# Rotary rotation run beside a projection's weight splits, keys turned in the retention's opening, and four side column tiles moved to the delta solve

## The reference, cut to what matters

```python
def rope(x, pos):
    ...
    x1, x2 = x[..., :half], x[..., half:]
    return jnp.concatenate([x1 * cos - x2 * sin, x2 * cos + x1 * sin], axis=-1)

q_b = rope(q_b.reshape(B, L, H_B, DK_B).astype(f32), pos)
k_b = rope(k_b.reshape(B, L, H_B, DK_B).astype(f32), pos) * (DK_B ** -0.5)
o_b, s_ret_new = retention(q_b, k_b, v_b, s_ret)
...
merged = (jax.nn.sigmoid(sel_a) * jnp.einsum('blv,vd->bld', o_a, w_br_a)
          + jax.nn.sigmoid(sel_b) * jnp.einsum('blv,vd->bld', o_b, w_br_b))
```

## Time and profile before

| | |
|---|---|
| median of 3 runs | 2276.4 us (2275.66 to 2284.68) |
| the profiled execution | 2275.99 us, its span 2274.1 us |
| PE busy | 1841.2 us, 81% of the span |
| DVE busy | 1303.4 us, 57% |
| ACT busy | 889.5 us, 39% |
| POOL busy | 639.1 us, 28% |
| DMA | 636.74 MB, mean 280 GB/s |

### The profile page before, as it was taken

One profiled execution on the slowest core, in us unless ns is written; L12 is line 12 of the kernel. 1 busy time (PEld: TensorE's weight loads), 2 busy tenths in 40 slices (PEclk: granted clock), 3 DMA queues, 4 the chain that ended last, 5 costly groups with the idle time before them and its releaser, 6 DMA issues.

```text
span 2274.1 us, 25972 instructions
## 1 busy us (share of the span) xinstructions
PE 1841.2 (81%) x8664; PEld 1184.0 (52%) x8664; DVE 1303.4 (57%) x2807; ACT 889.5 (39%) x2294; POOL 639.1 (28%) x558
## 2 busy tenths in 40 slices
PE   5989779979886986899997777777778777877776
PEld 4988679969766985655552222222223222322221
DVE  2227254451365524677667667676676867767664
ACT  4223212332224324354444544434444444444444
POOL 0002011000100002345444433444333444444442
PEclk9999789979897997999999999999999999999999
DMA  3313112253114235799999999999999999999997
GB/s 101 122 42 92 29 36 63 71 185 107 28 56 168 93 112 150 294 416 417 417 393 421 418 421 421 420 419 417 402 421 420 410 420 419 398 421 421 421 416 300
DMA packets 171783, 636.74 MB, mean 280 GB/s; under 512 B 12530, under 2 KB 97589, under 8 KB 104712
## 3 DMA queue, kind: packets, MB, share of 16 engines
q0 software_dynamic: 74880, 545.29, 58.1%
q1 hardware_dynamic: 96784, 89.98, 12.7%
HBM read 617.39 MB, written 17.93 MB: 279 GB/s over the span
## 4 chain that ended last, share of the span: by engine, by line
DMA 30%; PE 13%; DVE 8%; ACT 7%; issue 2%; POOL 0%; ACTq 0%; DVEq 0%
DMA ex_uv_row<-in_peer_uv,ex_eidx 30%; PE ps L1930 10%; DVE ex_uv_row L2093 4%; ACT L1976 2%; ACT ex_spread L1984 2%; ACT L1970 1%; ACT ret_tables L1981 1%; PE ps L571 1%; PE ps L573 1%; PE ps L572 1%; ACT ret_tables L1976 1%; DMA ex_uv_row<-in_peer_uv,ex_eidx_s 1%; DVE ex_sel L2065 0%; DVE ex_sel L2069 0%; DVE ex_best L2068 0%
## 5 line engine op out<-in xcount | busy, mean ns | idle before, releaser
L1930 PE MATMUL ps<-ex_uv_row,ex_spread 128*128 128x512 f32 (+1 forms) x2080 | 985.5, 609 | 264.1 <-ACT ex_spread L1984 260.4
L2093 DVE CUSTOM_DVE_ANT_0 ex_uv_row<-ex_uv_row,x_ffn 128x1024 f32<-128x1024 f32 x512 | 624.7, 1225 | 403.7 <-DMA ex_uv_row<-in_peer_uv,ex_eidx 398.9
L1930 PEld LDWEIGHTS ps<-ex_uv_row,ex_spread 128*128 128x128 f32 (+1 forms) x2080 | 363.1, 189 | 849.6 <-issue 849.4
L1892 POOL DMA_INDIRECT ex_uv_row<-in_peer_uv,ex_eidx x512 | 552.7, 1079 | 782.1 <-PE ps L1930 726.6
L1976 ACT ACTIVATE ret_tables<-ret_tables 128x1 f32<-128x1 f32 x520 | 104.7, 201 | 637.2 <-DVE ret_tables L2093 636.0
L1984 ACT ACTIVATE ex_spread<-square,ret_tables 128x128 f32<-128x128 f32 (+1 forms) x520 | 208.0, 400 | 17.0
L1981 ACT ACTIVATE ret_tables<-ret_tables 128x1 f32<-128x1 f32 x512 | 150.6, 294 | 17.0
L571 PE MATMUL ps<-proj_b_whi,x_lo 128*128 128x256 f32 (+1 forms) x320 | 91.1, 285 | 8.8 <-DVE proj_b_wlo L512 8.8
L571 PE MATMUL ps<-x_hi,ex_w_lo 128*128 128x260 f32 x256 | 84.7, 331 | 12.0 <-DVE ex_w_lo L2027 12.0
L573 PE MATMUL ps<-proj_b_whi,x_hi 128*128 128x256 f32 (+1 forms) x320 | 90.7, 284 | 0.0
L572 PE MATMUL ps<-proj_b_wlo,x_hi 128*128 128x256 f32 (+1 forms) x320 | 90.6, 283 | 0.0
(11 more groups left out here) (406 smaller groups left out, 3309.2 us busy)
## 6 DMA issues: line engine op xcount, KB each, us to landing
first_raw<-in_w_in SPq DMA_DIRECT2D x8, 1024.0 KB, 7.8
ex_uv_row<-in_peer_uv,ex_eidx POOLq DMA_INDIRECT x512
dp_w_raw<-in_w_in SPq DMA_DIRECT2D x10, 512.0 KB
proj_a_raw<-in_w_in SPq DMA_DIRECT2D x4, 1024.0 KB, 5.2
cv_w_raw<-in_w_in SPq DMA_DIRECT2D x8, 512.0 KB
proj_b_raw<-in_w_in SPq DMA_DIRECT2D x4, 1024.0 KB, 6.3
S_sample<-in_state_ret SPq DMA_DIRECT2D x1, 4096.0 KB, 22.3
out_ret_s<-S_sample SPq DMA_DIRECT2D x4, 1024.0 KB, 4.5
```

What stands on the lines that cost most here:

```text
L1892: pool.indirect_dma_start(uv_row[:, n % RING, :], None, a["peer_uv"][0], bass.IndirectOffsetOnAxis(ap=index_of(n), axis=0)).then_inc(row_l ...
L1930: ins = pe.matmul(k.pv[t % 2][0:r, c, :], spread[:, n % RING, 0:r], uv_row[:, n % RING, D + c * 512:D + (c + 1) * 512], start=first, stop= ...
L2093: dve.tensor_tensor_reduce(u, u, x, 1.0, 0.0, ALU.mult, ALU.add, coef[:, n:n + 1]).then_inc(dotted, 1)
```

## The change

It has three parts. `SIDE_BESIDE` becomes 2, 8 and 14: the phase `rotate` and its 4 tiles are gone, and `delta_solve` has 4 tiles more, 2 quarters in every slot of levels 1 to 6, with one ACT `take` in every slot. The rotation goes into DVE's list of `proj_b`: after the second split and after each later one, one of 8 rotations (the last two both after the last split), with `kb_tok` as scratch; the first waits for the loads of `qk_b` and `rope`. The transposes of the keys, their decay and the stacking of sample keys and values go into the opening of `retention`.

```diff
-SIDE_BESIDE = {"ba": 2, "cv": 8, "dp": 10, "rope": 4}
+SIDE_BESIDE = {"ba": 2, "cv": 8, "dp": 14}
@@ stream, vector
+                elif beside:
+                    each = [(*p, i, b) for p in plan() for i in range(p[0].steps) for b in range(2)]
+                    for n, chunk in enumerate(each):
+                        split(*chunk)
+                        if n == 1:
+                            for done in extra_done[0:2]:
+                                dve.wait_ge(done, 16)
+                        for work in (beside[n - 1:n] if n < len(each) - 1 else beside[n - 1:]) if n else ():
+                            work(own)
@@ delta_solve, tensor
-                            side.quarters(pe, 2 if n < 3 * NCH else 1)
+                            side.quarters(pe, 2)
@@ delta_solve, scalar
-                        if n < 2 * NCH or n % 2 == 0:
-                            if taken < side.halves:
-                                side.take(act, taken)
-                            taken += 1
+                        if taken < side.halves:
+                            side.take(act, taken)
+                        taken += 1
@@ rotate is replaced by
+def rotations(qk_b, rope, rot):
+    hh = P // 2
+    def rotate(n):
+        def work(own):
+            dve, x, sc = own.eng, qk_b[:, n, :], (1.0 if n < H else DK ** -0.5)
+            dve.scalar_tensor_tensor(rot[hh:P, 0, :], qk_b[0:hh, n, :], sc, rope[0:hh, 1, :], ALU.mult, ALU.mult)
+            dve.scalar_tensor_tensor(rot[0:hh, 0, :], qk_b[hh:P, n, :], sc, rope[hh:P, 1, :], ALU.mult, ALU.mult)
+            own.fence(dve.scalar_tensor_tensor(rot[:, 1, :], x, sc, rope[:, 0, :], ALU.mult, ALU.mult))
+            own.fence(dve.tensor_tensor(x, rot[:, 1, :], rot[:, 0, :], ALU.add))
+        return work
+    return [rotate(n) for n in range(2 * H)]
@@ retention, gpsimd
+                key_stack.on_gpsimd(pool)
+                value_stack.on_gpsimd(pool)
@@ retention, tensor
+                def turn_keys(t):
+                    out = k.pb[KEY_BANKS[t]] if t < NCH else sample_keys
+                    for h in range(H):
+                        ins = pe.transpose(out[0:ROWS[t], h * P:(h + 1) * P], qk_b[:, H + h, t * P:t * P + ROWS[t]], k.eye)
+                    ins.then_inc(keys_turned, 1)
                 scores(0)
+                for t in (NCH, 0, 1, 2):
+                    turn_keys(t)
                 ...
                 ins.then_inc(sample_mm, 1)
+                pe.wait_ge(keys_copied, 1)
+                turn_keys(NCH - 1)
                 ...
+                    else:
+                        pe.wait_ge(keys_copied, NCH)
+                        pe.wait_ge(dots_taken, 1)
                 ...
-                            pe.wait_ge(dots_taken, 1)
+                            pe.wait_ge(key_stacked, 1)
+                            pe.wait_ge(value_stacked, 1)
@@ retention, vector
                 decayed(0)
+                for t in range(3):
+                    decay_keys(t)
+                key_stack.on_vector(dve, sample_keys).then_inc(key_stacked, 1)
+                value_stack.on_vector(dve, sample_values).then_inc(value_stacked, 1)
                 ...
+                decay_keys(NCH - 1)
+                dve.wait_ge(value_stacked, 1)
                 dve.wait_ge(sample_mm, 1)
@@ retention, scalar
+                act.wait_ge(keys_turned, 1)
+                key_stack.on_scalar(act, sample_keys)
+                value_stack.on_scalar(act, sample_values)
+                act.wait_ge(key_stacked, 1)
                 states.on_scalar(act, 0)
```

More of the change, by code:

```diff
@@ L389, in stream @@
 @phase
-def stream(k, name, jobs, extra=(), first_raw=None, then=None):
+def stream(k, name, jobs, extra=(), first_raw=None, then=None, beside=()):
     nc = k.nc
@@ L1488, in _ @@
                     states.on_scalar(act, b)
[L1491 to L1532, removed]
-                                      k.pb[t % 2].rearrange("p (h d) -> p h d", h=H), head_bc(k.ret_kdec, P, P),
-                                      ALU.mult).then_inc(copied, 1)
-                key_stack.on_vector(dve, k.pb[0][0:NS, :]).then_inc(copied, 1)
-                dve.wait_ge(copied, NT)
-            @block.tensor
-            def _(pe):
-                side.quarters(pe, 2 * side.halves)
-                pe.wait_ge(roped, 2 * H)
-                for t, r in enumerate(ROWS):
-                    if t >= 2:
-                        pe.wait_ge(copied, t - 1)
-                    for h in range(H):
-                        ins = pe.transpose(k.pb[t % 2][0:r, h * P:(h + 1) * P], qk_b[:, H + h, t * P:t * P + r], k.eye)
-                    ins.then_inc(turned, 1)
@@ L1566, in retention @@
         key_of = k.sb("rs_key_of", [STACK, 2, QA], F32R, ctx)
+        key_stack, value_stack = Stack(k, "rs_keys", key_rows, True), Stack(k, "rs_values", value_rows, False)
+        keys_turned, keys_copied, key_stacked, value_stacked = (k.sem("rs_" + n) for n in
+            ("keys_turned", "keys_copied", "key_stacked", "value_stacked"))
+        sample_values, sample_keys = v_b[0:NS, NT - 1, :], k.pb[1][0:NS, :]
+        KEY_BANKS = (2, 3, 4, 2)
         qk_mm, a_done, own_s, os_mm, s_done, o_done, stored = (k.sem("rp_" + n) for n in
@@ L1588, in _ @@
                 wait(sp, early_loaded, 16 * len(early))
+            @block.gpsimd
+            def _(pool):
+                key_stack.on_gpsimd(pool)
+                value_stack.on_gpsimd(pool)
             @block.tensor
@@ L1607, in turn @@
                         ins.then_inc(turned, 1)
+                def turn_keys(t):
[3 more added lines that the diff above has]
+                    ins.then_inc(keys_turned, 1)
                 scores(0)
+                for t in (NCH, 0, 1, 2):
+                    turn_keys(t)
                 pe.wait_ge(sample_q, 1)
                 for h in range(H):
-                    ins = pe.matmul(k.pb[1][0:NS, h:h + 1], prod[:, h, :], k.ones[:, 0:1], start=True, stop=True)
+                    ins = pe.matmul(k.pb[5][0:NS, h:h + 1], prod[:, h, :], k.ones[:, 0:1], start=True, stop=True)
                 ins.then_inc(dots_mm, 1)
@@ L2194, in program @@
                     qk_b, rope = sb("qk_b", [P, 2 * H, T]), sb("rope", [P, 2, T])
+                    kb_tok = sb("kb_tok", [P, 4, QA])
+                    rot = flat(kb_tok)[:, 0:2 * T].rearrange("p (n t) -> p n t", n=2)
                     stream(k, "proj_b", [
@@ L2197, in program @@
                         Job(columns(w_in, COL_GATE_B, VB), 2, False, x_hi, x_lo, to_tokens(gate_b, VB), ACT.Silu)],
+                        beside=rotations(qk_b, rope, rot),
                         extra=[(qk_b[:, :, :], side_dram[:, 0:2 * H, :]),
@@ L2201, in program @@
                                 a["state_ret"][0].rearrange("b h k v -> k (b h) v"))], first_raw=raw0)
-                    kb_tok = sb("kb_tok", [P, 4, QA])
                     key_rows, value_rows = sb("rs_key_rows", [STACK, QA], F32R), sb("rs_value_rows", [STACK, VB], F32R)
-                    rotate(k, a, qk_b, kb_tok, rope, v_b, key_rows, value_rows)
                     retention(k, a, o, qk_b, v_b, kb_tok, S_sample, key_rows, value_rows, gate_b, x_hi, x_lo,
```

6 lines of the change are left out of this document (5 added, 1 removed).

## The result

The changed kernel takes 2257.0 us (median of 4 runs, 2254.0 to 2258.3) against 2276.7 before (median of 4 runs, 2275.7 to 2284.7); the ratio is 0.9904, 95% interval [0.9879, 0.9929], so it is faster by 19.6 us. Run once more on another occasion it took 2257.0 again, ratio 0.9906 [0.9889, 0.9922]. The prediction was 2258.5 in a range of 2252 to 2267.

What follows compares the result with a forecast made beforehand. PE and the DMA engines lead by turns; `rotate` (DVE 35.1, PE 28.9 of 42.8 us) stands between two barriers. -42.8 + 22.9 + 0 + 1.3 + 0.7 = -17.9 us gives 2258.5, range 2252 to 2267.

Steps and rivals of the forecast that it cites:

- The phase goes: `rotate` between two barriers: the retention opens where `rotate` did, -42.8 us, one barrier included (42.6 to 42.9).
- Four tiles: Delta solve, levels 3 to 6: 16 quarters at 1.43 us each, because PE never idles there, +22.9 us.
- DVE's collisions with POOL: Delta solve: four more POOL subtractions may stretch DVE; costed at nothing, up to 8.3 us if DVE's wait gave no cover.
- Rotation: Second projection: 8 rotations of 2.9 us on DVE fit its idle time ahead of the splits, 0 us.
- The opening: Retention's opening: 20 transposes +2.6 less 1.3 for the full clock, +1.3 us; the fourth decay not hidden, +0.7 us.
- The rule of the Trainium skill: Retention's opening: if transposes don't count as busy, the clock falls there and the sum is -16.2 us.
- Free tiles: Rival, delta solve: PE has gaps, so the side tiles cost nothing, 2235.6 us; chance 0.03.
- The serial opening: Rival, retention's opening: sample keys, stacks and fourth decay on the path, clock falls, +3.9 us, further fall +1.7: 2264.1; chance 0.10.
- The broken stream: Rival, second projection: each rotation holds up the next split, PE stops and the clock falls, +34.4 us, 2292.9; chance 0.05.

Runs made afterwards that it cites:

- experiment 1: Kernel before with only the four side tiles moved to the delta solve; rotation and keys stay in `rotate`: 2294.5 us, ratio 1.0064.
- experiments 2 and 6: 2: changed kernel with four side tiles not computed, 2237.4 us; 6: changed kernel with two or four late quarters moved behind chunks 1 to 3, 2245.8 or 2245.6.
- experiment 3: Changed kernel with the three products of every rotation done twice, 2260.0 us (2257.2 in one more run), or six times, 2281.4 us.
- Experiment 4: Changed kernel with key transposes, decays and stacks kept in a phase of their own ahead of the retention of before: 2269.0 us, ratio 0.9964.

## Why the prediction was right

*The phase goes, -42.8.* The retention opens at 631.22 instead of 651.14, 19.9 earlier; with +23.4 from the tiles and +0.7 from stages that the change doesn't touch, 44.0 went. 42.8 of it is the phase; 1.2 is in the projection, where the clock over the first 11.9 us was 0.73 instead of 0.61. I hadn't forecast this. It does not come from the projection's own edit: experiment 1, without that edit, has 0.73 too, and experiments 2 and 6, with it, have 0.61 to 0.62 and a projection of 119.6 to 119.8 us. All seven profiles with the changed kernel's delta solve have 0.73, so it may hang on what stands ahead; no run shows the cause. For the forecast this 1.2 us is luck.

*Four tiles, +22.9.* The slots gave 16 x 1.44 = 23.0, the stage 23.4. The choice to price a quarter by the difference of two kinds of slot, and not by the stage's busy share, is what made this right: the share of 85% would have promised room. Experiments 1 and 2 give the same price (22.2, 24.4) from both sides. DVE's collisions with POOL were costed at nothing, and none shows in the slots, where no DVE instruction takes over 0.7 us. The added subtractions fell beside no DVE instruction with two SBUF inputs, so DVE's wait as their cover was not put to the test. In the first part of the stage there are two that cost 1.7 and 1.9 us, the same as before the change.

*Rotation, 0.* Right, and right with a margin: twice the work cost nothing, and six times cost what the theory of experiment 3 gave. That theory was not quite the prediction's, which named 9.2 us of idle time ahead of a split as the point of decision. That is the row of the fourth split; later rotations have 11.8 us each (8.9 idle and their own 2.9), and the last two share 18.3 us, 9.2 each. At six times both this end and DVE's pace per chunk count, and what is lost is the excess over the cover and not the whole rotation.

*The opening, +1.3 and +0.7.* Measured +0.9 and +0.6 (PE's longer wait). The transposes came at 0.12 us each, and the clock stayed up. The rule of the Trainium skill, "TensorE: Matmul & The Clock Gate", Part 4, that transposes don't count as busy, would by the prediction's reading have let it fall here; the rows of 630 to 633 and 633 to 637 say 1.00 with 16 transposes in them. The measurement decides, for this place; that transposes count as busy elsewhere is not shown. What I had not forecast is that the retention as a whole stayed at 68.1 us: the loop gave 1.5 us back. One fall of the clock, the 0.67 from 680 to 685, worth 1.65 us, has no counterpart at the same distance behind the first chunk:

```profile
661.00:671.00 10.00, 8.33 (x48) 7.03 (x48) 7.44 (x22) 4.80 (x14) 0.00 (x0) 1.00 0.29 97
```

Such falls come and go: the stage took 67.7 to 69.7 us in kernels with the same loop that opened it at the upper clock. The sum was -17.9 and the medians moved by 19.6. In the profile, 1.2 and 1.5 us that no term had, 0.5 less in the opening, 0.5 more for the tiles and 0.7 more ahead of them make up the difference. So the mechanism was right, and that the time came out a little below the forecast is chance in the clock, inside the two falls of 1.7 us either way that the range allowed for.

*The rivals.* Free tiles fell by the slots. The serial opening fell: the first chunk starts where forecast. Experiment 4, which puts the same work in a phase of its own with a barrier and the value stack ahead, cost 10 to 12 us; the rival's 3.9 for an opening without that barrier was not tried. The broken stream fell by the splits' idle time and by experiment 3.

## What to carry to other kernels

Price work that is moved into a stage by the difference between two neighbouring pieces of that stage with and without it; the stage's mean idle time lies elsewhere, here nearly all in the first 68 of its 176 us, and that is where the work belonged (11 us more). A phase between two barriers costs its longest engine plus its serial head and tail, so emptying it pays even when a part of its work gets dearer on the way: here tiles that had cost 8 us cost 23, and the sum was still -20. Before an engine's idle time is used as cover, find the place where two pieces share one stretch; here it was the end. A profile is one execution: stages of the same code differed by 1 to 6 us between these profiles (delta solve 198.7 to 201.1, retention 67.7 to 69.7, retrieval 1403.2 to 1409.5), so a difference of 2 or 3 us is read from slots and waits, not from a stage or a time.

## What the runs showed of the hardware

More work can shorten a stretch: 72 products more in the first part of the delta solve made it 5.4 us shorter, with the granted clock up from 0.77 to 0.86. A short pause behind a dense stage left the clock alone: PE stopped for 1.2 us and the clock stayed at 1.00, in the changed opening and in experiment 4, and fell in experiment 4 only in the pause of 4.50 us that followed. A DVE instruction with two SBUF inputs took 2.07 to 2.84 us beside a POOL subtraction and 0.69 to 0.70 without. The Trainium skill, "SBUF — State Buffer", "Who interferes with whom", tells of this exclusion, and the traces agree; a DVE subtraction with one input in PSUM took 0.69 us inside a POOL subtraction (389.8 us of the kernel before).
